# Projections laid between the steps of an attention layer, on one core of a Trainium2 chip

## The reference

```python
qa, qb, ka, kb, va, vb = split(h_lat @ w_in)          # 8 + 8 query heads, 2 + 2 key heads, 2 + 2 value heads
qb = rms_norm(qb, q_norm);  kb = rms_norm(kb, k_norm)  # group B only
qa, ka, qb, kb = [apply_axial_rope(t, rope) for t in (qa, ka, qb, kb)]
k_c, v_c = h_ctx @ w_in[:, Q_WIDTH:]                   # the context gives keys and values alone
o_a = window_attention(qa * scale, ka, va, ka_c, va_c, sink)   # |i-j| <= 128, all context keys, a sink logit
o_b = global_attention(qb * scale, [kb_c, kb], [vb_c, vb])     # all 512 keys
x = x + g1 * (concat(o_a, o_b) @ w_out)
x = x + g2 * (square(relu(modulate(rms_norm(x)) @ w1)) @ w2)
```

## Time and profile before

| | us |
|---|---|
| median of 3 runs (range) | 2731.54 (2729.57 to 2732.7) |
| the profiled execution, its span | 2730.95, 2729.2 |
| mean granted TensorE clock over the span | 0.963 of full |
| busy: PE, DVE, ACT | 2526.8, 1995.0, 1120.9 |
| PE matmuls of the units' lines L356, L365 in the chain that ended last | 47% and 24% of the span |

### The profile page before, as it was taken

The page is one execution under the profiler, slowest core; times in us unless marked ns, Lnnn a source line. Parts: engine busy times, 40 slices in busy tenths (PEclk is TensorE's granted clock), DMA queues, the critical chain, the costliest instruction groups (busy, mean ns, idle before and its releaser), DMA issues.

```text
span 2729.2 us, 41835 instructions
## 1 busy us (share of the span) xinstructions
PE 2526.8 (93%) x13492; PEld 2111.7 (77%) x13492; DVE 1995.0 (73%) x2373; ACT 1120.9 (41%) x1494; POOL 0.2 (0%) x4
## 2 busy tenths in 40 slices
PE   7869987797999999999979999999899999999996
PEld 2338884476788888888868788787688888888885
DVE  6788758777987878878768888878675565565654
ACT  2224225643444444444434334233344444444442
POOL 0000000000000000000000000000000000000000
PEclk9989997898999999999999999999899999999998
DMA  8857843474998888888858567576556666666662
GB/s 312 301 187 264 298 159 108 139 259 165 314 311 278 283 278 279 276 283 280 274 172 280 182 226 257 167 252 201 176 181 189 187 190 185 190 186 188 189 185 92
DMA packets 441695, 608.80 MB, mean 223 GB/s; under 512 B 18363, under 2 KB 387228, under 8 KB 439580
## 3 DMA queue, kind: packets, MB, share of 16 engines
q1 hardware_dynamic: 440188, 598.53, 66.9%
q10 hardware_dynamic: 1440, 9.44, 0.9%
HBM read 597.41 MB, written 10.49 MB: 223 GB/s over the span
## 4 chain that ended last, share of the span: by engine, by line
PE 82%; DVE 11%; issue 3%; ACT 2%; DMA 2%; DVEq 0%; SPq 0%; ACTq 0%
PE ps L356 47%; PE ps L365 24%; PE ps L1114 2%; DVE w_lo L395 1%; PE ps L663 1%; PE ps L929 1%; DVE acc L407 1%; PE ps L893 1%; DMA raw<-in_mlp_w 1%; PE ps L1124 1%; DVE hm L715 1%; DVE hm L723 1%; DMA raw<-in_mod_w 1%; DVE lat L729 1%; DVE sm L1508 1%
## 5 line engine op out<-in xcount | busy, mean ns | idle before, releaser
L395 DVE TENSOR_TENSOR w_lo<-raw,w_hi 128x1024 fp32r<-128x1024 f32 x720 | 877.2, 1224 | 523.5 <-ACT w_hi L391 519.3
L391 ACT ACTIVATE w_hi<-raw 128x1024 fp32r<-128x1024 f32 x720 | 760.0, 1060 | 1056.2 <-PE ps L365 892.2
L356 PE MATMUL ps<-lat,w_hi 128*128 128x512 f32 x3200 | 839.2, 399 | 65.6 <-DVE lat L729 58.5
L356 PEld LDWEIGHTS ps<-lat,w_hi 128*128 128x128 f32 x3200 | 587.3, 192 | 177.5 <-issue 49.7
L356 PE MATMUL ps<-alt,w_hi 128*128 128x512 f32 x2688 | 698.2, 395 | 7.8 <-DVE mod L419 5.7
L356 PEld LDWEIGHTS ps<-alt,w_hi 128*128 128x128 f32 x2688 | 488.1, 190 | 96.7 <-DVE mod L419 6.0
L365 PEld LDWEIGHTS ps<-lat,w_lo 128*128 128x128 f32 x3200 | 448.7, 192 | 32.0 <-DVE w_lo L395 0.4
L365 PE MATMUL ps<-lat,w_lo 128*128 128x256 f32 x3200 | 464.1, 284 | 0.0
L365 PEld LDWEIGHTS ps<-alt,w_lo 128*128 128x128 f32 x2688 | 374.7, 191 | 25.8
L365 PE MATMUL ps<-alt,w_lo 128*128 128x256 f32 x2688 | 389.1, 283 | 0.0
L407 DVE SCALAR_TENSOR_TENSOR acc<-slab,silu,acc 128x1024 f32<-128x1024 f32 x300 | 381.4, 1279 | 5.9 <-DMA slab<-in_mod_w 2.4
(11 more groups left out here) (180 smaller groups left out, 1411.6 us busy)
## 6 DMA issues: line engine op xcount, KB each, us to landing
raw<-in_mlp_w SPq DMA_DIRECT2D x512, 512.0 KB, 3.8
slab<-in_mod_w SPq DMA_DIRECT2D x352, 512.0 KB, 6.0
raw<-in_hy_w_in SPq DMA_DIRECT2D x96, 512.0 KB, 6.3
raw<-in_attn_w_in SPq DMA_DIRECT2D x48, 512.0 KB, 6.1
raw<-in_mod_w SPq DMA_DIRECT2D x32, 512.0 KB, 7.4
raw<-in_attn_w_out SPq DMA_DIRECT2D x32, 512.0 KB, 4.8
raw<-in_hy_w_out SPq DMA_DIRECT2D x32, 512.0 KB, 6.6
spec_dram<-spec ACTq DMA_DIRECT2D x8, 1024.0 KB, 7.8
```

The source lines that it names most:

```text
L356: e.matmul(ps[:, bank, :], w_hi[:, n % RING, kk, fb * P:(fb + 1) * P], t[:, kb, :], start=(kb == 0), stop=False)
L391: e.activation(w_hi[:, n % RING], raw[:, n % RING], ACT.Copy).then_inc(hi_ready, 1)
L395: e.tensor_tensor(w_lo[:, n % RING], raw[:, n % RING], w_hi[:, n % RING].bitcast(F32), ALU.subtract).then_inc(split_ready, 1)
```

## The change

Query iteration 0 is computed first (`T_Q0`), then the keys (`T_K`), then the values (`T_V`), which get a form of their own. The attention's 32 steps are written as 37 with a table `UNIT_AT` that puts one projection unit ahead of a step on PE: 24 units of the queries' iterations 1 to 3, and 6 of the 8 units of the first output iteration, in an order (`OUT_ORDER`) that needs the late heads last. `SPLIT_AT` puts the units' splits on ACT and DVE four steps earlier.

```diff
-        T_Q, T_KV, T_OUT, T_MLP0 = 1, 5, 7, 11
+        T_Q0, T_K, T_V, T_Q, T_OUT, T_MLP0 = 1, 2, 3, 4, 7, 11
...
+        UNIT_AT = {**{s_: s_ for s_ in range(26)}, 28: 26, 29: 27, 31: 28, 33: 29}
+        SPLIT_AT = {**{s_: s_ + 4 for s_ in range(-4, 26)}, 28: 30, 29: 31, 31: 32, 33: 33}
+        STEPS = 37
+        def pair_at(s_, late):
+            p = (s_ - late - 3) // 4 + 2
+            return p if (s_ - late - 3) % 4 == 0 and 2 <= p < 8 else None
...
+            for s_ in range(STEPS - 1):
+                if s_ in UNIT_AT:
+                    woven_unit(UNIT_AT[s_])
+                pe_step(s_)
+                if s_ == 32:
+                    e.wait_ge(exp_done, 31)
+                    pe_close(e, M_OUT, FIN_ATT, 4)
+            woven_unit(30)
+            woven_unit(31)
+            with e.Fori(1, 4) as i:
+                pe_iter(e, T_OUT + i, alt, lambda j: (head_ready, 2 + HEADS), None, (2, i - 1))
```

```diff
+            def swap_pair(p):
+                if p < 4:
+                    e.wait_ge(psum_free, pair_done(p))
+                else:
+                    e.wait_ge(b_scaled, p - 1)
+                if p < 2:
+                    e.wait_ge(kq_sums, 1)
+                else:
+                    e.wait_ge(q_v, 3 * (p - 2) + 3)
+                for b in range(4):
+                    e.dma_start(q_swap[32 * (b ^ 1):32 * (b ^ 1) + 32, p % 2], q_pair(p)[32 * b:32 * b + 32]
+                                ).then_inc(q_swapped[p % 2], 16)
...
+                p = pair_at(s_, 1)
+                if p is not None and p >= 4:
+                    e.wait_ge(psum_free, pair_done(p))
+                    e.wait_ge(kq_sums, p - 3)
+                    e.activation(q_sq[:], q_pair(p), ACT.Square).then_inc(q_squared, 1)
+                p = pair_at(s_, 2)
+                if p is not None and p >= 4:
+                    act_root(e, p - 1, 4)
...
+                p = pair_at(s_, 1)
+                if p is not None and p >= 4:
+                    e.wait_ge(q_squared, p - 3)
+                    e.tensor_scalar(q_pair(p), q_pair(p), qn, None, ALU.mult).then_inc(b_scaled, 1)
+                p = pair_at(s_, 2)
+                if p is not None and p >= 4:
+                    rs = rs_q[:, 4 * p:4 * p + 4]
+                    dve_rsqrt(e, p - 1, ps[:, 2 * (p % 2), 0:4], 4, 1.0 / HEAD, EPS * QSCALE * QSCALE, rs, (kq_sums, p - 2))
+                    e.tensor_scalar(rs, rs, QSCALE, None, ALU.mult).then_inc(k_v, 1)
+                p = pair_at(s_, 3)
+                if p is not None:
+                    rotate_pair(p)
```

```diff
+                for kk in range(2):
+                    kb = 2 * n + kk
+                    for part in range(2):
+                        for tb, bank in enumerate(V_BANKS):
+                            act = (lat, alt)[tb // 2][:, kb, ds(part * TOK + tb % 2 * P, P)]
+                            e.matmul(ps[:, bank, :], act, hi[:, kk, :], start=(kb == 0 and part == 0), stop=False)
...
-        M_Q = 0
-        M_KV, M_ATT = M_Q + 4, M_Q + 12
+        M_KV, M_ATT = 0, 8
         M_OUT = M_ATT + 8
-        M_MLP0 = M_OUT + 4
+        M_MLP0 = M_OUT + 8
```

More of the change, by code:

```diff
@@ L383, in pe_finish, with pe_close @@
                                      acc[:, h, b * P:(b + 1) * P], ident)
+            mm.then_inc(mod_cols, 1)
+        def pe_close(e, sl_count, fin, bank):
+            e.wait_ge(slabs_used, 4 * sl_count + 4)
+            for h in range(2):
+                for b in range(half):
+                    at = h * half + b
+                    mm = e.matmul(ps[:, bank, at:at + 1], acc[:, h, b * P:(b + 1) * P], ones[:, 0:1],
+                                  start=True, stop=True)
             mm.then_inc(mod_cols, 1)
@@ L609, in dve_iter @@
                     dve_norm_lo(e, norm[0], norm[4], n)
-                if ctx_chunk is not None and n == 5:
-                    dve_norm_lo(e, 1, alt, ctx_chunk)
+                if n in ctx:
+                    dve_norm_lo(e, 1, alt, ctx[n])
                 if after_unit:
@@ new lines, in _ @@
+            for m in range(34):
+                woven_unit(m)
+                if m == 2:
+                    swap_pair(0)
+                    swap_pair(1)
+                if m >= 4:
+                    slab_step(e, sp_slabs, m - 4)
+                if pair_at(m - 8, 1) is not None:
+                    swap_pair(pair_at(m - 8, 1))
+            slab_step(e, sp_slabs, 30)
+            slab_step(e, sp_slabs, 31)
+            woven_unit(34)
+            sp_slabs(e, SL_OUT, 0, 0, 1)
+            woven_unit(35)
@@ L998, in _ @@
-            e.wait_ge(rs_v, 6 * 2 + 6)
-            e.wait_ge(v_ready, 4)
-            for h in range(2):
-                for c in range(4):
-                    mm = e.matmul(ps[:, h, c * P:(c + 1) * P], rs_k[:, 4 * h + c:4 * h + c + 1].to_broadcast([P, P]),
-                                  ident, start=True, stop=True)
-            mm.then_inc(k_spread, 1)
-            e.wait_ge(k_v, 6)
-            def swap_pair(pair):
-                if not isinstance(pair, int) or pair:
-                    e.wait_ge(q_v, 3 * pair)
-                e.matmul(ps[:, 0, :], swap, q[:, ds(2 * pair, 2), :], start=True, stop=True).then_inc(q_swapped, 1)
@@ new lines, in _ @@
+            first = FirstOut(G1, 0, OUT_0)
+            for n in range(2, 8):
+                dve_split(e, T_OUT + 1, n)
+                if n in (2, 3):
+                    first.dve_head(e, T_OUT, n - 2)
+                if n >= 4:
+                    dve_slabs(e, SL_OUT, 1, 2 * (n - 4), 2)
+                if n == 7:
+                    Gated(G1, 1, OUT_0).dve_head(e, T_OUT + 1, 0)
+            with e.Fori(2, 4) as i:
+                dve_iter(e, T_OUT + i, Gated(G1, i - 1, OUT_0), Gated(G1, i, OUT_0), i, SL_OUT)
```

650 lines of the change are left out of this document (367 added, 283 removed).

## The result

| | before | after |
|---|---|---|
| median, us (range) | 2730.56 on this chip | 2705.88 (2704.05 to 2707.89) |
| ratio after / before | | 0.9904, 95% interval 0.9889 to 0.992 |
| span of the profiled execution | 2729.2 | 2706.1 |
| mean granted TensorE clock | 0.963 | 0.966 |
| busy: PE, DVE, ACT | 2526.8, 1995.0, 1120.9 | 2515.8, 1983.3, 1125.0 |

Faster by 1.0%, some 25 us, where the forecast was 45. The time lies in the range of 2662 to 2712 and the direction was right, but a little over half of the gain came. The range was wide enough for two rivals: the 2675 to 2697 that the forecast gave to its own mechanism misses by 9 us, and the time lies in the 2695 to 2707 of the second rival.

A forecast was written before the change was run, and what follows sets the result against it. No engine was full in the old attention; ACT, DVE and PE waited for each other. Replacing 425.6 us by 97.0 + 203 + 72.5 + 5.2 + 1.5 = 379.2 gave 2686 us against 2731.54, range 2662 to 2712.

The forecast's parts named there:

- the second rival: Attention steps: no unit hides any wait and swaps come late, 203 to 212 + 12 us; 2700 us, chance 0.22.
- the head: Keys, values and closes, from the queries' end to the attention steps: PE full, 97.0 us in place of 124.6.
- The ring: Attention steps: split, mask, exponential and scaling form a loop through ACT and DVE, 5.25 us a step; chance 0.50.
- the rival with PE as the bound: Attention steps: ACT and DVE run ahead, so PE's 163 + 8 us set the time; 2654 us, chance 0.18.
- One sign: Expected in the waits of the attention steps: PE's scores wait for the exponential's end.
- rotation +1.3: Every fourth attention step: a pair's rotation on DVE delays the next split by 1.3 us, six times.
- root +2.7: Group B's steps: DVE waits for ACT's table load and inverse root, adding 2.7 us, four times.
- the term of 3 us: Attention steps: allowance of 3 us for units that run at a slow TensorE clock behind waits.
- The tail: From score 31 to unit 30, the last steps with the close, one unit and the last product: 18.5 us.
- my +1.6: Group B's steps: DVE waits for ACT's squares before scaling the pair, adding 1.6 us, four times.
- late swaps: Attention steps: the pairs' swap transfers might need 13 us and hold up rotations; six pairs add 12 us.
- The slow clock as a state for the whole stretch: Woven attention steps: TensorE falls to 1.2 GHz and stays, PE's 163 us become 326; 2809 us, chance 0.05.

The follow-up runs named there:

- e1: The changed kernel with DVE's split of unit s + 4 moved from ahead of the mask to behind the reciprocal: 2683.01 us, ratio 0.9811.
- e3: The changed kernel with DVE making a head's low half right behind the reciprocal, ahead of rotation and slab: 2696.00 us, ratio 0.985.
- e10: e7 with DVE accumulating only 32 of 1024 columns in the steps' 32 slabs: 2655.82 us, ratio 0.9715.
- e6: The changed kernel with the close behind step 33 and DVE's gate sums and last slabs one step later: 2702.33 us, ratio 0.9882.
- e5: The changed kernel with group B's square root replaced by an exponential, so ACT keeps its table: 2706.06 us, ratio 0.9897.
- e9: The changed kernel without the SBUF transfers that swap the pairs, their semaphore raised instead: 2701.42 us, ratio 0.9875.
- e8: The changed kernel with units and splits in blocks of four ahead of every fourth step, not woven: 2738.56 us, ratio 1.0021.
- e7: The changed kernel with the edits of e1, e3 and e6 together, low half ahead of the split: 2664.12 us, ratio 0.9732.

## Why the prediction was right and wrong

**The direction and the head: right.** The 30 us of the earlier trace rows became nothing, and keys and values with their closes took 99.9 us for 97.0. Of the 2.9 us too much, 1.92 is PE's wait ahead of unit 0 for DVE's last read-out of the values (L549). I had put no wait there. The other 1 us came before the keys: the queries' iteration 0 ends at 227.1 us in place of 226.0.

**The ring: right in mechanism, and nearly right in price.** It took 5.10 us around in the trace for my 5.25, and e1 takes it away. That shortened the stretch by 22.4 us, to 201.0, which is still 30 us above the 171 of the rival with PE as the bound. One sign was wrong: the scores never waited on PE for the exponential.

**The step that failed: "It is a ring through both engines" was taken for the only tie.** I wrote down for each extra DVE operation what it delays in the ring (rotation +1.3, root +2.7), and did not ask what the last operation of DVE's list, the low half of a head, is waited for by. PE's product used to alternate between two PSUM banks and now has one. This wait costs 28.2 us of PE's idle time in 12 places; e3 takes 20.4 us of it away, and 14 to 15 us show at the end. 18.8 us of the 28.2 lie in the three middle rows of the table, which are 6.6 us too long together, 7.6 in the first, where other errors hid them, and 1.8 in the tail.

**A unit left out: 5.3 us.** My head ended where unit 0 starts, and my steps began with score 0, so unit 0 stands in neither sum. This is an error of counting and no mechanism, and it is a fifth of the 25.6 us between the forecast's 379.2 and the measured 404.8.

**The slow clock: the term of 3 us was mis-sized.** PE's work in the stretch was put at 163 us. e10, at clock 0.98, has it busy for 164.4 us, so the count of matmuls was right. In the changed kernel the same 992 instructions take 183.2 us at clock 0.90: 19 us more. I had said that waits would be under 1 us in most steps and up to 3 in the root steps; there were twelve for the low half alone, up to 5.9 us. Behind six of them the product ran at about half speed (3.50 to 3.76 us for 1.95; granted clock 0.55 in the one shown), behind the other six at full speed (2.02). A part of these 19 us may only have filled time that PE would have waited for anyway, so they are not to be added to the waits; no run tells how large that part is.

**The tail: 29.7 us for 18.5.** I priced the close at its 3.4 us, and it took 6.34, as it waited 1.97 for the last slab and then ran at the slow clock. And the last head's low half stands behind four slabs, with 2.52 us of waiting for a transfer. Both are order alone, and the e6 trace gives back 10 us. With 11.2 us this row is the largest single part of what was missed.

**Small terms.** DVE waited 2.0 us each time for the squares (I had 1.56 + 0.6) and 2.7 for the root (I had 1.56 + 1.5), with the load inside at 1.28 and no drain (e5). What they add to a step, my +1.6 and +2.7, no run takes apart. The transfers were in time (e9), so the second rival's "late swaps" is refuted; its other half, that no unit hides a wait, does not fit e8, where the same work in blocks takes 32 us more. Its number, 2700, was still the nearest of all to 2705.88, since its 128 us for the bare steps was far too little (some 174 in e8): the right size for a wrong reason. I held it at 0.22, and the ring, whose own range missed, at 0.50; that the time fell into the common range says nothing for the ring. The first rival, PE as the bound with 163 + 8 us, describes not this kernel but e7 (a stretch of 175.9 us) and e10 (168.2). The slow clock as a state for the whole stretch did not come; the mean was 0.90.

**Left open.** Two banks for the products, the direct test of the bank theory, was not tried. That e3 and e1 act through just these two waits rests on the waits of their traces. Each stretch is from one execution, and differences of a few us between traces (e10 against e7) are not settled by it. How much of the tail's 10 us reaches the median is not settled.

## What to carry to other kernels

When work is laid between the steps of another loop, list for every engine the order of one whole step, and for each operation ask who waits for it, the last one above all. Work that is prepared four steps early, here the split, should not stand ahead of the operation that the loop waits for, and a read-out that frees a single bank should not stand behind bulk work. Moving these two operations, with nothing taken out, gave 39 us, more than the restructuring itself had given. A wait of TensorE is to be priced with what its clock does behind it, not by its length alone.

## What the hardware showed that I had not expected

- The close, 32 matmuls with one column, takes 3.63 us at full clock (behind the values in the changed kernel, and in the steps of e6), 0.113 each, and 6.34, 0.198 each, at a granted clock of 0.55. The 0.106 that I had from the earlier trace rows and called a slow-clock price was one at full clock: the granted clock was 1.00 while those matmuls ran (401.0 to 402.7 us of the kernel before) and 0.50 under the spread (408.9 to 412.7). A mean clock of 0.76 over a stretch doesn't say at which level one of its groups ran.
- The length of the wait just ahead does not by itself tell the level: behind 1.83 us (541.55 us) the product ran at full clock in 2.02 us, behind 1.51 in e6 the same product took 3.75. In the changed kernel four products came behind a wait of 1.09 us: one took 3.54 us, three took 2.02.
- The table load of ScalarE shows no drain: 0.02 us ahead of it and 0.01 behind it.
